# One kernel for a mixer block and an attention block: order of the head rounds in the second branch

## Reference

```python
qk = silu(causal_dwconv(ml_qk, ml_conv_w, ml_conv_b))        # 4 taps, per channel
# per head, with b = cumsum(log_f), m_t the running maximum (computed over the whole sequence in the kernel):
s     = (q @ k.T) * exp(logD - m_t)                          # masked to the past
num   = s @ v
den   = sum(s, axis=-1)
denom = maximum(abs(den), exp(-m_t))
h     = num / denom
y_ml  = rmsnorm(h, ml_norm_g) * sigmoid(ml_o)                # mean of squares over 256 values
...
mixed = gates[0] * (y_hg @ w_br_hg) + gates[1] * (y_ml @ w_br_ml) + gates[2] * (y_mb @ w_br_mb)
```

## Time and profile before

| | |
|---|---|
| median of 3 runs | 1533.23 us (1533.01 to 1534.1) |
| profiled execution, its own time | 1534.11 us |
| its span | 1532.3 us |
| PE busy | 1514.5 us of the span |
| DVE, ACT, POOL busy | 820.7, 727.7, 667.9 us |
| granted TensorE clock over the span | full speed (1.0) in nearly all of it |
| rounds 1 to 3 and the tail of the branch | from 437.25 us to about 542 us of the span |

### The profile page before, as it was taken

One profiled execution on the slowest core, in us unless ns is written; L12 is line 12 of the kernel. 1 busy time (PEld: TensorE's weight loads), 2 busy tenths in 40 slices (PEclk: granted clock), 3 DMA queues, 4 the chain that ended last, 5 costly groups with the idle time before them and its releaser, 6 DMA issues.

```text
span 1532.3 us, 20919 instructions
## 1 busy us (share of the span) xinstructions
PE 1514.5 (99%) x7180; PEld 1238.7 (81%) x7180; DVE 820.7 (54%) x1392; ACT 727.7 (47%) x1164; POOL 667.9 (44%) x509
## 2 busy tenths in 40 slices
PE   7999999999999999999999999999999999999999
PEld 6888888888887778888878888888888887777777
DVE  4677778342257742576642445555552245756761
ACT  6667665323345442466654344444443244545551
POOL 5433333444543554433344444444455544433432
PEclk9999999999999999999999999999999999999999
DMA  6222222222322123222223323333333343232212
GB/s 244 83 70 74 78 69 72 94 96 84 95 83 70 57 95 96 83 83 69 70 83 96 97 96 97 96 96 96 98 98 105 109 128 113 75 101 93 79 59 96
DMA packets 39399, 140.87 MB, mean 92 GB/s; under 512 B 4312, under 2 KB 4824, under 8 KB 39328
## 3 DMA queue, kind: packets, MB, share of 16 engines
q1 hardware_dynamic: 37664, 134.89, 27.6%
q10 hardware_dynamic: 1664, 5.01, 0.9%
HBM read 137.76 MB, written 2.13 MB: 91 GB/s over the span
## 4 chain that ended last, share of the span: by engine, by line
PE 95%; DVE 3%; issue 1%; ACT 1%; DMA 0%; SPq 0%; DVEq 0%
PE bank L504 26%; PE bank L508 26%; PE bank L507 26%; PE bank L732 3%; PE bank L1020 3%; PE bank L605 1%; PE bank L759 1%; PE bank L939 1%; PE bank L929 1%; PE bank L920 1%; DVE m L2068 1%; PE bank L658 0%; DVE unit L1837 0%; PE bank L1011 0%; DMA xs<-x 0%
## 5 line engine op out<-in xcount | busy, mean ns | idle before, releaser
L445 POOL TENSOR_TENSOR wl<-raw,wh 128x512 fp32r<-128x512 f32 x490 | 647.8, 1344 | 839.9 <-ACT wh L1063 827.6
L504 PE MATMUL bank<-hh,wh 128*128 128x512 f32 x840 | 333.5, 397 | 3.8 <-DVE unit L1837 3.8
L508 PE MATMUL bank<-hh,wl 128*128 128x512 f32 x840 | 327.7, 390 | 0.0
L507 PE MATMUL bank<-hl,wh 128*128 128x512 f32 x840 | 327.2, 390 | 0.0
L504 PE MATMUL bank<-yh,wh 128*128 128x512 f32 x800 | 314.6, 393 | 0.4 <-DVE au L2329 0.4
L1063 ACT ACTIVATE wh<-raw 128x1024 fp32r<-128x1024 f32 x241 | 252.9, 1051 | 125.3 <-DMA raw<-slabs 124.6
L508 PE MATMUL bank<-yh,wl 128*128 128x512 f32 x800 | 311.5, 389 | 0.0
L507 PE MATMUL bank<-yl,wh 128*128 128x512 f32 x800 | 311.4, 389 | 0.0
L504 PEld LDWEIGHTS bank<-hh,wh 128*128 128x128 f32 x840 | 157.9, 188 | 37.5 <-POOL wl L445 5.5
L508 PEld LDWEIGHTS bank<-hh,wl 128*128 128x128 f32 x840 | 157.6, 188 | 34.0
L507 PEld LDWEIGHTS bank<-hl,wh 128*128 128x128 f32 x840 | 158.0, 188 | 31.4
(11 more groups left out here) (355 smaller groups left out, 2033.4 us busy)
## 6 DMA issues: line engine op xcount, KB each, us to landing
raw<-slabs SPq DMA_DIRECT2D x245, 512.0 KB, 3.5
xs<-x SPq DMA_DIRECT2D x4, 512.0 KB, 5.9
xT<-xt SPq DMA_DIRECT2D x4, 512.0 KB, 12.7
wb<-bias_scratch ACTq DMA_DIRECT2D x1, 1792.0 KB, 7.7
wb<-bias_scratch ACTq DMA_DIRECT2D x2, 896.0 KB, 4.4
out<-a_l SPq DMA_DIRECT2D x4, 256.0 KB, 4.7
out<-au SPq DMA_DIRECT2D x3, 256.0 KB, 2.0
con<-consts ACTq DMA_DIRECT2D x1, 767.0 KB, 7.1
```

Source lines behind the costliest of these rows:

```text
L445: pool.tensor_tensor(slab(wl, i, half), slab(raw, i, half), slab(wh, i, half).bitcast(F32), ALU.subtract).then_inc(S["slab_split"], 1)
L504: mm(bank[:, :], wh[:, s, b, :], xh, start=first and i == 0, stop=False)
L507: mm(bank[:, :], wh[:, s, b, :], xl, start=False, stop=False)
L508: ins = mm(bank[:, :], wl[:, s, b, :], xh, start=False, stop=last and i == len(order) - 1)
```

## The change

The same instructions run, in another order, on three engines; POOL's and SP's lists are the same.

```diff
@@ PE
                 ml_scores(u)
+                project(nxt + 2)
                 ml_finish(u - 1)
-                project(nxt + 2)
                 project(nxt + 3)
                 ml_values(u)
@@ ACT
                 slab_hi(nxt + 4)
+                ml_round(u)
+                ml_sums(u)
                 ml_rms(u - 1)
-                ml_round(u)
-                ml_hi(u - 1)
-                ml_sums(u)
                 if not last:
                     silu_tables()
+                ml_hi(u - 1)
+                if not last:
                     ml_silus(u + 1)
-                    act.wait_ge(S["ml_y"], 4 * u)
@@ DVE, ml_sums is cut in two
+            def ml_sums_rest(u):
                 dve.wait_ge(S["ml_ps"], 6 * u + 5)
                 TT(m_pl[:, :], m_ps[:, :], m_ph[:, :].bitcast(F32), ALU.subtract).then_inc(S["ml_ps"], 1)
@@ DVE, ml_ratio
-                wait(dve, S["ml_dn"], 3 * u)
@@ DVE, the rounds
-                ml_ratio(u - 1)
+                ml_ratio(u - 1, lambda: conv(0))
                 ml_diag(u)
                 ml_add_rest(u - 1)
-                conv(0)
                 conv(1)
                 ml_weights(u)
+                ml_sums(u)
                 ml_y(u - 1)
-                ml_sums(u)
+                ml_sums_rest(u)
                 ml_lo(u - 1)
```

More of the change, by code:

```diff
@@ L2172, in _ @@
             ml_sums(0)
+            ml_sums_rest(0)
             rest_v(1)
```

## The result

The changed kernel takes **1536.16 us** (median of 20 runs, 1535.03 to 1537.12), the kernel before 1533.64 in its own 20 (1532.91 to 1535.64): ratio 1.0016, interval 1.001 to 1.0023, 2.5 us more. The profiled execution has 1536.47 us and a span of 1534.7, 2.4 over the span before.

A forecast was written before the change was run, and what follows sets the result against it. PE, busy 99%, can win only idle time, bound by a loop through PE, DVE and ACT. Waits of 6.7 us against 5.5 add 1.2 to a 1533.2 median: 1534.4 us; eight-in-ten range 1531.0 to 1536.9.

The forecast's parts named there:

- Convolution: First slab's convolution moved ahead on DVE: ends at R + 9.19; PE stalls 0 in round 2, 0.58 us in round 3.
- R: The start of `ml_ratio` on DVE in a round, from which the prediction counts its times in us.
- Additions beside POOL: Four DVE additions ahead of the scalings meet POOL's `m_ql`: taken as 4.55 us, in place of 1.48.
- C: Length of the four additions on DVE: taken as 4.55 us, bounds 1.48 and 5.12.
- Norm's factor: `ml_rms` on ACT, queued behind `m_ph`: ready at R + 22.40; `ml_values` waits 1.34 us in round 2, 1.58 in round 3.
- first slab of round 3: PE waits 0.45 us there for the bank that ACT's gate of `nxt+2` gives.
- Length of a round: From R to the next R: 31.79 us, in place of 31.55; ACT's chain gains nothing.
- Tail: PE's wait before the last `ml_finish`: 2.77 us, being 1.34 plus 1.43 more.
- The step that failed: Sum of PE's waits in the branch: 6.7 us after against 5.5 before, so 1.2 us more.
- The forecast: Stalls move from the convolutions to `ml_values` and the tail and cancel out: 1534.4 us, own range 1532.5 to 1536.1, chance 0.78.
- the first: Rival: the additions do not meet POOL, convolution stalls vanish and no other comes: 1529.0 us, chance 0.10.
- the second: Rival: more contention with POOL than at head 0, C up to 6.0, slower by over 0.2%, 1538.8 us; chance 0.12.

The follow-up runs named there:

- no_ql: The changed kernel without POOL's three `m_ql` subtractions for heads 1 to 3, PE reading `m_qh` instead: 1529.1 us against 1533.84 for the kernel before.
- rms_first: The changed kernel with the norm's factor on ACT moved ahead of `m_ph`, the copy of the weights' sums: 1529.41 us against 1533.84 for the kernel before.
- sums_back: The changed kernel with the four additions back behind the scalings, and on ACT factor, `ml_hi`, then `m_ph`: 1533.08 us against 1533.84 for the kernel before.
- mid_pause: The kernel before with the second step of head 2's denominator (0.72 us) made once more: 1535.19 us against 1533.74.
- tail2: The kernel before with the second step of the last head's denominator made two times more: 1536.78 us against 1533.84.
- rms_tail2: The changed kernel with the factor ahead of `m_ph` and the last head's denominator step made two times more: 1532.06 us against 1533.73 for the kernel before.
- mid_long2: The kernel before with one unread 128x512 DVE instruction added ahead of round 3's `conv(0)`: 1534.98 us against 1533.84.

## Why the prediction was right, and where it was not

**Convolution.** Predicted to end at R + 9.19; it did, to the hundredth. The stall in round 2 is gone, the one in round 3 is 0.38 (from the last of L691 to L504 0.62 where round 2 has 0.24; too short to be drawn as a wait), predicted 0.58.

**Additions beside POOL.** C taken as 4.55, measured 4.48 in round 1. `no_ql` shows the cause.

**Norm's factor.** `ml_values` waits 1.34 in round 2 (1.18 and the 0.17), predicted 1.34, and 1.71 in round 3, predicted 1.58. `rms_first` shows that its place behind `m_ph` is the whole of it. The first slab of round 3 waits 0.49, predicted 0.45.

**Length of a round.** R to R 31.83, predicted 31.79.

**Tail.** 2.69 (the page of waits has 2.5, the row 2.54), predicted 2.77. Together 1.34 + 0.49 + 0.38 + 1.71 + 2.69 = 6.6, predicted 6.7; before 5.5. The net, predicted 1.2, is 1.1 by these and 1.14 by the two timelines.

**The step that failed** is the last one, "After: 1.34 + 0.45 + 0.58 + 1.58 + 2.77 = 6.7; before: 5.5. 1.2 us more". That sum takes PE's idle time for all that PE loses. It has no term for what a pause does to the matmuls behind it, and the tail's pause, put rightly at 2.77, was longer than any that before has in the branch (2.28 from start to start, in round 3). With 1.6 for the clock it would have been 2.8 and 1536.0, beside the 1536.16 measured. The forecast was 1534.4, so it had under half of the 2.5 us. The result lies at the end of the forecast's own range, 1536.1, but for another reason: that end stood for C = 5.12. That the range held is in this part luck.

**The rivals.** The additions did meet POOL, which speaks against the first. They took 4.48, under the 5.2 from which the second decides.

**What stays open.** What decides whether the low clock comes. In the recorded executions full clock stands behind pauses of 2.28 (before), 2.29 (`sums_back`) and 2.54 (`mid_pause`), half clock behind 2.69 (after), 2.77 (`tail2`), 2.78 (`rms_tail2`) and 2.92 (`mid_long2`). That looks like a border, but each is one execution, and by the mean granted clocks of the others one kernel goes both ways. It is 1.0 in 1 of 20 executions of after, and that one is the fastest, 1535.03. It is 1.0 in 3 of 11 of `rms_tail2`, 4 of 11 of `mid_pause` and 3 of 11 of `mid_long2`, and 0.999 in 15 of the 87 of the kernel before that ran beside the experiments. Where a low stretch lies in those executions was not recorded, and 0.999 by itself proves none: in `sums_back` the 3 of 11 that have it are the fastest. Nor is a long pause enough: in before PE's first matmul comes 9.25 us behind the start of the span, and from 8 to 36 us the granted clock is 1.00. So a pause of 2.7 to 2.9 us brings the stretch in most executions here, and the price of 1.6 us is one to be weighed with a chance.

## What to carry to other kernels

Before a small instruction is moved ahead on one engine, look at what is queued behind its reader on the next one: here a factor whose last input came at 455.90 and 485.08 (L574, rounds 1 and 2 of after) was begun only at 458.89 and 490.70, behind a sum that nobody needed yet, and one line moved on ACT turned a loss of 2.5 us into a gain of 4.4. Price a stall on TensorE twice, once as idle time and once by the clock granted behind it; several short pauses can be cheaper than one long one of the same sum. And look at the granted clock of all executions, not only at the one whose trace is read. And two instructions that meet on a shared path should be judged by who waits for them, not by how long they are drawn.

## What the runs showed of the hardware

**TensorE's clock behind a pause.** In the four traces with a pause of 2.69 to 2.92 us in the branch, matmuls of 128x512 started every 0.43 us instead of 0.23 for 3.4 us, beginning 1.1 to 1.3 us behind the first matmul (542.10 and 543.20 in after, 512.97 and 514.09 in `mid_long2`). The stretch was 3.4 us long each time, whatever the pause, and cost 1.6 (0.43 is less than twice 0.228, so it is not half of 3.4). Other executions of the same kernels seem to go without it, as said above.

**DVE and POOL take turns.** The four additions are 0.22, 0.55, 0.42 and 0.29 us alone (`sums_back`, round 2, as before the change) and 0.71, 1.66, 1.40 and 0.72 beside POOL's subtractions. The Trainium skill says in "SBUF — State Buffer", section "SBUF: two separate sides", that the pair of ports that VectorE and GpSimd share is locked for a whole instruction, and that the other engine blocks. These rows agree: the middle two grow by 1.11 and 0.98, most of one subtraction of POOL (1.24, a third of 3.73), and not in proportion to their own size. Convolution taps, which read a bank, keep their time beside POOL: three take 2.31 at 448.05 of before, with POOL at work from 447.36 on, and 2.31 at 444.67 of after, where POOL starts only at 449.27.

**The start of the branch wanders.** Among the profiled executions round 1 began between 436.2 and 437.5 us, in code ahead of it that is the same in all of them. With differences of 1 or 2 us, two spans are better compared from the first instruction of the part that was changed.
